# Last tile of a sparse-attention step: ScalarE counts one of four rows of the threshold search, and every selection mask is made before attention

## What is computed

```python
def _prompt_attention(q, qi, wi, k, v, kidx):
    def blk(args):                         # one block of 128 queries
        qb, qib, wib, pos = args
        sc = _index_scores(qib, wib, kidx)
        sc = jnp.where(key_pos[None, None, :] <= pos[None, :, None], sc, NEG_INF)
        _, idx = lax.top_k(sc, topk)       # topk = 256
        valid = idx <= pos[None, :, None]
        return _sparse_attend(qb, _gather_rows(k, idx), _gather_rows(v, idx), valid)
```

## Time and profile before

| | us |
|---|---|
| median of three executions | 3211.51 |
| the three executions | 3210.68 to 3214.54 |
| span of the profiled execution, first to last instruction | 3205.7 |
| its mean granted TensorE clock | 0.996 of full speed |
| PE busy | 3116.2 (97%) |
| DVE busy | 1984.1 (62%) |
| ACT busy | 1160.8 (36%) |
| POOL busy | 961.8 (30%) |

### The profile page before, as it was taken

One profiled execution on the slowest core, in us unless ns is written; L12 is line 12 of the kernel. 1 busy time (PEld: TensorE's weight loads), 2 busy tenths in 40 slices (PEclk: granted clock), 3 DMA queues, 4 the chain that ended last, 5 costly groups with the idle time before them and its releaser, 6 DMA issues.

```text
span 3205.7 us, 47659 instructions
## 1 busy us (share of the span) xinstructions
PE 3116.2 (97%) x18495; PEld 2706.4 (84%) x18495; DVE 1984.1 (62%) x3862; ACT 1160.8 (36%) x2080; POOL 961.8 (30%) x869
## 2 busy tenths in 40 slices
PE   7999999999999999999999999999999999999999
PEld 6999999967987888888888888889888788887887
DVE  5443695054635993057257999078446999948862
ACT  3444332355324221155244221165326321136651
POOL 3345665454510332023201331111300232025310
PEclk9999999999999999999999999999999999999999
DMA  9765688685874655722744556600663555640026
GB/s 315 254 210 194 224 272 282 242 282 167 301 235 150 207 189 206 236 98 103 257 158 155 199 196 215 227 28 11 254 199 128 177 191 197 229 164 9 11 75 230
DMA packets 266530, 599.32 MB, mean 187 GB/s; under 512 B 17693, under 2 KB 177623, under 8 KB 216130
## 3 DMA queue, kind: packets, MB, share of 16 engines
q1 hardware_dynamic: 255796, 558.38, 51.0%
q0 software_dynamic: 10368, 37.75, 3.5%
q10 hardware_dynamic: 142, 0.13, 0.0%
HBM read 453.65 MB, written 142.57 MB: 186 GB/s over the span
## 4 chain that ended last, share of the span: by engine, by line
PE 87%; DVE 6%; ACT 2%; POOL 2%; DMA 1%; issue 1%; SPq 0%; ACTq 0%; DVEq 0%; POOLq 0%
PE ps L1236 81%; PE ps L1241 6%; DVE PTL L2259 1%; DVE SC L2051 1%; DVE RS L2010 1%; DMA MW<-in_w_mod 1%; POOL PTL L2624 1%; POOL BBL L2677 0%; DVE LP L2276 0%; ACT PTH L1104 0%; DMA WR<-in_w_proj_b 0%; ACT SC L987 0%; DVE PFX L2156 0%; DMA WR<-in_w_in 0%; DVE BD L2155 0%
## 5 line engine op out<-in xcount | busy, mean ns | idle before, releaser
L1236 PE MATMUL ps<-HTH,WLH 128*128 128x512 f32 x3504 | 1129.2, 391 | 0.0
L1236 PEld LDWEIGHTS ps<-HTH,WLH 128*128 128x128 f32 x3504 | 658.2, 188 | 138.9 <-issue 5.0
L1236 PE MATMUL ps<-HTL,WLH 128*128 128x512 f32 x1752 | 683.0, 390 | 0.0
L2117 DVE TENSOR_SCALAR_CACHE_REDUCE JUNK<-SC,SMALL 128x384 bf16<-128x384 f32 (+13 forms) x392 | 580.0, 1480 | 15.6 <-POOL sSC L2556 1.7
L1236 PE MATMUL ps<-H,WLH 128*128 128x288 f32 x3504 | 481.1, 298 | 3.8 <-POOL H L2529 2.6
L1236 PEld LDWEIGHTS ps<-H,WLH 128*128 128x128 f32 x3504 | 471.6, 190 | 5.8 <-issue 2.5
L2276 DVE CUSTOM_DVE_ANT_0 LP<-ps,SC,RQ 128x512 f32<-128x512 f32 (+3 forms) x320 | 202.6, 666 | 320.0 <-ACT SC L987 275.2
L1236 PEld LDWEIGHTS ps<-HTL,WLH 128*128 128x128 f32 x1752 | 329.4, 188 | 64.9
L946 ACT ACTIVATE T<-ps 128x512 f32<-128x512 f32 x192 | 114.8, 598 | 707.1 <-PE ps L1236 705.5
L2470 POOL TENSOR_TENSOR WLH<-WR,WLH 128x1024 fp32r<-128x1024 f32 x97 | 235.4, 2427 | 311.4 <-ACT WLH L768 311.3
L2051 DVE SCALAR_TENSOR_TENSOR SC<-T,WI,SC 128x512 f32<-128x512 f32 (+3 forms) x266 | 179.8, 700 | 120.1 <-ACT T L880 119.6
(11 more groups left out here) (367 smaller groups left out, 5224.5 us busy)
## 6 DMA issues: line engine op xcount, KB each, us to landing
WLH<-w_scratch SPq DMA_DIRECT2D x291, 1024.0 KB, 4.9
w_scratch<-WLH SPq DMA_DIRECT2D x97, 1024.0 KB, 5.6
WR<-in_w_in SPq DMA_DIRECT2D x73, 512.0 KB, 4.4
MW<-in_w_mod SPq DMA_DIRECT2D x6, 2048.0 KB, 16.3
q_scratch<-QO SPq DMA_DIRECT2D x32, 256.0 KB, 5.6
ma_scratch<-T SPq DMA_DIRECT2D x32, 256.0 KB, 5.6
gb_scratch<-GB SPq DMA_DIRECT2D x32, 256.0 KB, 5.6
QU<-q_scratch SPq DMA_DIRECT2D x64, 128.0 KB, 2.2
```

Source lines behind the costliest of these rows:

```text
L1236: return pe.matmul(out, lhsT, rhs, start=start, stop=stop, **more)
L2117: ins_ = dve.tensor_scalar(JUNK[0:n, 0:row.shape[1]], row, MID[0:n, c:c + 1], 0.0, ALU.is_ge, ALU.add, accum_out=CNT[0:n, c:c + 1])
```

## The change

1. In the last tile, the counts of row block 3 (2048 columns, 28 steps) go from DVE to ACT: `shared_count` takes the sign of MID minus score and accumulates it. A step's MID is handed over by `mid_set`, the sum comes back by `tally`. ACT does step s after PROJ_B item 4 + 3 * (s // 2) + s % 2, that is after items 4, 5, 7, 8, 10, 11 and so on to 43, 44.
2. There are no late blocks any more: select chooses all four blocks of the last tile before attention. `piece_mask`, POOL's `probabilities_low` and ACT's PTW copy go; all low halves of the probabilities are made on DVE.
3. ACT makes the bias of block b right after PROJ_B item 58 + b in tiles 1 and 2 and after item 60 + b in tile 3, and no longer after item 63. Tile 0 stays as it was.
4. For the last unit `lengths` runs its first product with the start flag off.

```diff
+    shared_block = lambda t: BLOCKS - 1 if t == TILES - 1 else None
+    SEARCH_AFTER = {4 + 3 * (step // 2) + step % 2: step for step in range(STEPS)}
+    mask_after = lambda t, i: i - (len(PROJ_B) - (4 if t == TILES - 1 else 6))
...
+        def shared_count(t, step):
+
+            b = shared_block(t)
+            n = width(BLOCKS * t + b)
+            act.wait_ge(*mid_set.at(t, step))
+            if step:
+                act.wait_ge(*tally.at(t, step - 1))
+            act.activation(COUNTED[:, 0:n], SC[:, b, 0:n], ACT.Sign,
+                           bias=MID[:, b:b + 1], scale=-1.0, accum_out=SIGNS).then_inc(*tally.mark(t, step))
...
-            if t and low_on_pool(t, u, c):
-                act.activation(PTW[slot][:, 0:m], src, ACT.Copy).then_inc(*p_copy_a.mark(t, u, c, 'raw'))
...
+                elif mask_after(t, i) in range(BLOCKS):
+                    block_mask(t, mask_after(t, i))
+                if shared_block(t) is not None and i in SEARCH_AFTER:
+                    shared_count(t, SEARCH_AFTER[i])
                 j += 1
-            masks(t)
             if t == 0:
+                masks(t)
                 both_attentions()
...
-                          part_ == 0, part_ == 1, skip_group_check=True)
+                          part_ == 0 and u + 1 < len(UNITS), part_ == 1, skip_group_check=True)
...
             for step in range(STEPS):
                 for row, n, c, name in rows:
+                    if name == shared:
+                        continue
...
+                    own = slice(c0, shared)
+                    dve.scalar_tensor_tensor(TAKEN[:, own], CNT[:, own], float(TOPK), RANGE[:, own], ALU.is_ge, ALU.mult)
+
+                    dve.wait_ge(*tally.at(t, step))
+                    both = slice(shared, shared + 1)
+                    link(dve.scalar_tensor_tensor(TAKEN[:, both], SIGNS, float(width(BLOCKS * t + shared) - 2 * TOPK), RANGE[:, both],
+                                                  ALU.is_le, ALU.mult))
...
+                        ins_.then_inc(*mid_set.mark(t, step + 1))
+                        dve.wait_ge(*mid_set.at(t, step + 1))
...
-                if name not in late_blocks(t):
-                    for r in range(len(pieces(row.shape[1]))):
-                        choose(t, row, n, c, name, r)
+                for r in range(len(pieces(row.shape[1]))):
+                    choose(t, row, n, c, name, r)
...
-            if low_on_pool(t, u, c):
-                return
...
-                for b, r in late_runs(t, u):
-                    band_of(t, scores(t)[:, b, 0:width(BLOCKS * t + b)], P, b, b, r)
                 for c in range(4, groups):
                     probabilities_low(t, u, c)
-                for b, r in late_runs(t, u):
-                    needed_of_band(t, scores(t)[:, b, 0:width(BLOCKS * t + b)], P, b, b, r)
```

More of the change, by code:

```diff
@@ L348, in program @@
     RANGE, LOW = ps[7][:, 256:261], ps[7][:, 264:269]
+    COUNTED = at("COUNTED", [P, SEQ], BF16, rKH)
+    SIGNS = small(88, 1)
     rows_in = signal("rows_in", 16)
@@ L435, in program @@
     gb_out, gb_in = signal("gb_out", 16), [signal(f"gb_in{i}", 16) for i in range(2)]
-    v_low, diag, late_mask, p_low_dve, p_low_pool = (
-        signal(n) for n in ("v_low", "diag", "late_mask", "p_low_dve", "p_low_pool"))
+    v_low, diag, p_low_dve = signal("v_low"), signal("diag"), signal("p_low_dve")
     vl_out, vl_in = signal("vl_out", 16), [signal(f"vl_in{i}", 16) for i in range(2)]
+    mid_set, tally = signal("mid_set"), signal("tally")
     bb_high, bb_low_pool, bb_low_dve = signal("bb_high"), signal("bb_low_pool"), signal("bb_low_dve")
@@ L980, in block_mask @@
             row = scores(t)[:, b, 0:width(BLOCKS * t + b)]
-            if b in late_blocks(t):
-                act.wait_ge(*late_mask.at(t, b, 3))
-                act.activation(row, row, ACT.Copy, bias=NEG, scale=-NEG).then_inc(*biased.mark(t, b))
-                return
             act.wait_ge(*mask.at(t, b))
@@ L990, in masks @@
             for b in index_blocks(t):
-                if b not in late_blocks(t):
-                    block_mask(t, b)
+                block_mask(t, b)
+        def shared_count(t, step):
[6 more added lines that the diff above has]
+                           bias=MID[:, b:b + 1], scale=-1.0, accum_out=SIGNS).then_inc(*tally.mark(t, step))
         def sample_mask():
@@ L2114, in select @@
             dve.wait_ge(*causal.at(t))
+            shared = shared_block(t)
+            if shared is not None:
+                link(dve.memset(MID[:, cs], 0.0))
+                dve.memset(MID[:, shared:shared + 1], 0.0).then_inc(*mid_set.mark(t, 0))
             for step in range(STEPS):
                 for row, n, c, name in rows:
+                    if name == shared:
+                        continue
                     ins_ = dve.tensor_scalar(JUNK[0:n, 0:row.shape[1]], row, MID[0:n, c:c + 1], 0.0, ALU.is_ge, ALU.add,
@@ L2119, in select @@
                     link(ins_)
-                link(dve.scalar_tensor_tensor(TAKEN[:, cs], CNT[:, cs], float(TOPK), RANGE[:, cs], ALU.is_ge, ALU.mult))
+                if shared is None:
+                    link(dve.scalar_tensor_tensor(TAKEN[:, cs], CNT[:, cs], float(TOPK), RANGE[:, cs], ALU.is_ge, ALU.mult))
+                else:
+                    own = slice(c0, shared)
[4 more added lines that the diff above has]
+                                                  ALU.is_le, ALU.mult))
                 link(dve.scalar_tensor_tensor(LOW[:, cs], TAKEN[:, cs], 2.0 ** -step, LOW[:, cs], ALU.mult, ALU.add))
                 if step + 1 < STEPS:
-                    link(dve.scalar_tensor_tensor(MID[:, cs], HI[:, cs], 2.0 ** -(step + 1), LOW[:, cs], ALU.mult, ALU.add))
+                    ins_ = dve.scalar_tensor_tensor(MID[:, cs], HI[:, cs], 2.0 ** -(step + 1), LOW[:, cs], ALU.mult, ALU.add)
+                    if shared is None:
+                        link(ins_)
+                    else:
+                        ins_.then_inc(*mid_set.mark(t, step + 1))
+                        dve.wait_ge(*mid_set.at(t, step + 1))
             link(dve.tensor_copy(LO[:, cs], LOW[:, cs]))
@@ L2130, in select @@
             for row, n, c, name in rows:
-                link(dve.tensor_scalar(JUNK[0:n, 0:row.shape[1]], row, HI[0:n, c:c + 1], 0.0, ALU.is_ge, ALU.add,
+                link(dve.tensor_scalar(JUNK[0:n, 0:row.shape[1]], row, HI[0:n, c:c + 1], 0.0, above(t, name), ALU.add,
                                        accum_out=CNT[0:n, c:c + 1]))
@@ L2135, in select, with above @@
             for row, n, c, name in rows:
-                if name not in late_blocks(t):
-                    for r in range(len(pieces(row.shape[1]))):
-                        choose(t, row, n, c, name, r)
+                for r in range(len(pieces(row.shape[1]))):
+                    choose(t, row, n, c, name, r)
+        def above(t, name):
+            return ALU.is_gt if name == shared_block(t) else ALU.is_ge
         def choose(t, row, n, c, name, r):
@@ L2149, in band_of @@
             x, g, band, pre = row[:, a:a + m], GT[0:n, 0:m], BD[0:n, 0:m], PFX[0:n, 0:m]
[L2150 to L2154, removed]
+            link(dve.tensor_scalar(g, x, hi, None, above(t, name)))
             link(dve.scalar_tensor_tensor(band, x, lo, g, ALU.is_ge, ALU.subtract))
@@ L2161, in needed_of_band @@
             x, g, band, pre = row[:, a:a + m], GT[0:n, 0:m], BD[0:n, 0:m], PFX[0:n, 0:m]
-            late = name in late_blocks(t)
             if r + 1 < len(runs):
                 link(dve.tensor_copy(CNT[0:n, c:c + 1], PFX[0:n, TILE - 1:TILE]))
[L2165 to L2169, removed]
+            link(dve.scalar_tensor_tensor(band, pre, need, band, ALU.is_le, ALU.mult))
             ins_ = dve.scalar_tensor_tensor(x, band, -1.0, g, ALU.add, ALU.add)
@@ L2603, in first_value_halves @@
             pool.tensor_copy(VR[:, 2 * f:2 * f + 2, :], high.bitcast(F32)).then_inc(*v_low.mark(0, f))
[L2605 to L2609, removed]
         def diagonals(t, u):
@@ L2616, in diagonals @@
                                R4[u % 2].unsqueeze(2).to_broadcast([P, 4, P]), ALU.mult).then_inc(*diag.mark(t, u))
[L2618 to L2625, removed]
         def branch_low(f):
```

18 lines of the change are left out of this document (2 added, 16 removed).

## The result

The changed kernel takes 3185.11 us (median of four executions, 3181.93 to 3186.41) against 3213.03 for the kernel before beside it. The ratio is 0.9912, with a 95% interval of 0.9898 to 0.9926: faster by about 28 us, where 28.2 were forecast. The profiled span went from 3205.7 to 3180.1 us, by 25.6.

A forecast was written before the change was run, and what follows sets the result against it. PE sets the pace, but late masks and their POOL detour hold attention's units 0 to 8 in the last tile. Gains 22.1 + 2.9 + 2.7 + 0.5 = 28.2 us off 3211.5 give 3183.3; range 3178 to 3193.

The forecast's parts named there:

- A count of 2.2 us: Last tile's search: one block 3 count on ACT, priced like an exponential over 2048 columns with its sum.
- 2837.3 forecast: Last tile: time at which DVE's search and all four blocks' masks end, against attention's start at 2859.97.
- the cover: Between the last mask's end and attention's start in the last tile: 22.7 us left.
- the 6.0 us limit: Last tile's PROJ_B: a count on ACT may take 6.0 us before PE feels it.
- The rival in which ACT becomes the bound: PROJ_B: counts over 6.0 us, at 7.3 with four load times, hold PE by full banks; 3219.7 us, chance 0.03.
- the upper bound: Units 0 to 8 of tile 3: tile 2's 78.23 us plus another step of 29.92 gives 108.15.
- the middle: Units 0 to 8 of tile 3: 105.0 us, taken between 101.6 and 108.15.
- The lower bound: Units 0 to 8 of tile 3 by PE's work, 0.935 us a key block: 101.6 us.
- the first interval: First unit mark interval of tile 3's attention: estimated 0.8 us shorter, with no unit to finish yet.
- Without part 1 it would be none (2859.9): Last tile, all counts on DVE: masks would end at 2859.9, leaving no time before attention's start at 2859.97.
- The working: Last tile's choosing: 1.13 us a key block; blocks 2 and 3, with 31 key blocks, take 35 us.
- the query load: Starts of attention in tiles 1 and 2: landing late, it could take back up to 1 us in each.

The follow-up runs named there:

- parts 2 to 4 without part 1: The changed kernel with all four blocks counted on DVE, masks still before attention: 3189.71 us, ratio 0.9925 to the kernel before.
- the three kernels that keep the late masks: The kernel before with only the earlier bias, only block 3's count on ACT, or only all low halves on DVE: ratios 0.9978, 1.0003, 0.9997.
- the low halves on DVE: The kernel before with all low halves on DVE, none on POOL, late masks still in attention: 3211.06 us, ratio 0.9997.
- four passes: The changed kernel with each of ACT's counts run four times, extra sums unused: 8.5 us a count, ratio 1.0068 to the kernel before.
- moving both low halves: The changed kernel with DVE making the fourth and fifth low halves before finishing the previous unit, where groups are five: 3180.72 us, ratio 0.9897.
- Part 3 alone: The kernel before with only the bias of blocks that are not late moved ahead of item 63: 3208.91 us, ratio 0.9978.
- the second trace of the same kernel: The changed kernel profiled once more with no edit: 3181.19 us, ratio 0.9901 to the kernel before, span 3177.5.
- Part 1 alone: The kernel before with only block 3's counts moved to ACT, late masks still in attention: 3214.21 us, ratio 1.0003.

## Why the prediction was right

**What bounded the kernel.** The late masks held PE in units 0 to 7: shown by parts 2 to 4 without part 1 (units at 104.6 us) and by the three kernels that keep the late masks (124.4, 120.0 and 124.9 us between DGs). The prediction named the masks and POOL's detour together; the low halves on DVE show that DVE's work is the larger part and that the detour alone gives back nothing that the time shows.

**Part 1.** A count of 2.2 us was taken from the exponential; it is 2.0 + 0.19, 2.1 as they overlap. ACT's slots set the pace (the waits in one step of two), and the last choose starts at 2836.56, which puts the end at 2837.25, 2837.3 forecast. Attention comes earlier than it was reckoned with, so the cover is 20.9 us (block 3's mask is at 2858.12) and not 22.7. PE loses nothing. Against the row, the 6.0 us limit was too careful by at least 0.4 us; it entered no term of the sum. The rival in which ACT becomes the bound exists and ends slower (four passes), but needs 8.5 us a count. Its condition was given as 6.0, its cause as table loads: there are none beside the counts, and two for each would not have been enough.

**Part 2.** 104.6 us against 105.0, between the bounds of 101.6 and 108.15; marks of 12.4 to 13.5 (12.3 to 13.6 forecast), no stretch at 0.66 near 2880. The mechanism was right: tile 2's wait for a low half does not come back with seven groups (no wait of PE from 2860 to 2976). In tile 2 it is there, and moving both low halves gives 3.2 us; from the 74.99 without it the upper bound's own step, 29.92, leads to 104.9. That the middle hit to 0.4 us is luck, though. The lower bound was meant as PE's own work, and it was 3.0 us too low: with no wait left, PE is busy for all 104.4 us between the DGs. Units of 13 key blocks take about 12.8 us (12.4 reckoned), those of 14 take 13.4 (13.2), and the first interval, 12.64 us from R4R, is not 0.8 shorter. So 104.6 is no middle between waiting and not waiting; it is what PE needs with nothing to wait for.

**The worth of part 1.** "Without part 1 it would be none (2859.9)" left attention just in time. It is worse: the last choose ends at 2863.97. The working counted 1.13 us a key block for blocks 2 and 3 as for 0 and 1, 35 us in all. Without part 1 they take 41.5 us (2822.5 to 2864.0), in the changed kernel 36.8 (2800.4 to 2837.3). POOL makes its key halves at the end of PROJ_B, from 2827.5 and 2826.3 on, so beside most of the one and beside the last 11 us of the other. Scans of 512 columns that overlap them take 2.19 us (2828.12 without part 1, 2833.55 in the changed kernel), those with POOL idle 1.28 (2797.65 and 2861.17 without part 1). That POOL's work is the cause is argued from this overlap; no run moves it. So part 1 is worth 0 us alone and 6.6 us under part 2, by 4.1 us of PE's wait and about 2.5 us of low clock behind it. That is by the marks of one execution of each; the ratios (0.9925 against 0.9912 and 0.9901) say 4 to 8.

**Part 3.** Tile 1 gave 2.28 us, not 2.9: the transposes start at 1394.18 as forecast (1394.3), but 0.45 of that was won before item 63, and ACT then waits 0.97 us for the query load that the prediction named as able to take back up to 1, with the high halves queued behind it. That fits the rest of the gap; no run tests it. Tile 2 gave 2.78 (2.7), tile 3 0.33 (0.5). Part 3 alone gave 2.2 and 2.8 in the same places.

**Sum.** The terms measured are 22.43 + 2.28 + 2.78 + 0.33 = 27.8 us, against 28.2. The span shrank by 25.6 only, the median by 27.9. What lies between the terms and the span are the other rows of the table above, most of it low clock in other places of a single profiled execution; the second trace of the same kernel has a span of 3177.5, which is the forecast to the digit by chance.

## What to carry to other kernels

Work that is late inside a stage bound by TensorE can cost more than its busy time: here it came with waits of PE and its weight loads and with one to four stretches at the low clock. Move it into the cover of the stage before, and then find the engine with room there, whose own worth shows only together with the move (0 us alone, 6.6 with it). How much a helper engine may take is read from its average work between two items that the bound engine hands it, with the buffers between them as slack, and runs with the work doubled, tripled and quadrupled bracket it. Rows of neighbouring tiles hold such an estimate to a few us. Here the step from tile to tile, added to a tile without its wait, came nearest (104.9 for 104.6); one unit scaled down by key blocks came out 3 us short.

## What the runs showed of the hardware

- Sign with a sum over 2048 columns takes 1.99 + 0.19 us on ACT, as long as the exponential of that size, and in no kernel here did it bring a table load: neither between evacuations nor between an exponential and a Silu.
- A low-clock stretch of 1.7 us' loss shortly after attention ends (1499 to 1507 and 2506 to 2518) stands at one or both places in 9 of the 13 executions profiled, and at none in 4, before's among them. Part 1 alone, with the old attention, has both, so they don't come from the new attention. In the changed kernel PE had idled ahead of both, busy 2.89 of 5 us from 1495 to 1500 and 0.93 of 3 from 2504 to 2507; but in the kernel before PE idled at the same points of its work too (2.66 of 5 from 2506 to 2511), and the clock stayed at 1.00. What sets them off is open.
- After the wait of 4.1 us, without part 1, PE stayed at 1.2 GHz for 5.6 us more; after waits of up to 1.2 us in the earlier trace rows it fell once, with part 3 alone four times. Which waits do it these runs don't tell.
